# Residual, normalised and transposed rows and split latents moved by 64 bytes in on-chip memory, in a two-layer decoder trunk

## What is computed

```python
cond = jax.nn.silu(c)
for layer in range(DEPTH):
    mod = (cond @ ada_w[layer] + ada_b[layer])[:, None, :]
    sh_m, sc_m, g_m, sh_f, sc_f, g_f = jnp.split(mod, 6, axis=-1)
    h = _rmsnorm(x, gn[0]) * (1.0 + sc_m) + sh_m
    y = _stick_breaking(h, ...)      # layer 0;  _mla(h, ...) in layer 1
    x = x + g_m * _rmsnorm(y, gn[1])
    h = _rmsnorm(x, gn[2]) * (1.0 + sc_f) + sh_f
    y = _swiglu(h, ...)              # layer 0;  _moe(h, ...) in layer 1
    x = x + g_f * _rmsnorm(y, gn[3])
```

## Time and profile before

| | |
|---|---|
| runs | 819.71, 819.73, 819.80 us |
| profiled execution, span from first to last instruction | 818.9 us (its own time is not listed apart; the median of the runs is 819.73) |
| TensorE matmuls, busy | 796.3 us, 97% |
| weight loads / VectorE / ScalarE / GpSimd busy | 708.9 / 694.0 / 542.3 / 48.9 us |
| granted TensorE clock, mean | 0.994 of 2.4 GHz |
| DMA | 284.31 MB, mean 347 GB/s |

### The profile page before, as it was taken

One profiled execution on the slowest core, in us unless ns is written; L12 is line 12 of the kernel. 1 busy time (PEld: TensorE's weight loads), 2 busy tenths in 40 slices (PEclk: granted clock), 3 DMA queues, 4 the chain that ended last, 5 costly groups with the idle time before them and its releaser, 6 DMA issues.

```text
span 818.9 us, 12488 instructions
## 1 busy us (share of the span) xinstructions
PE 796.3 (97%) x4678; PEld 708.9 (87%) x4678; DVE 694.0 (85%) x587; ACT 542.3 (66%) x575; POOL 48.9 (6%) x54
## 2 busy tenths in 40 slices
PE   4999999999999999999999999999999999999995
PEld 4999788999999888999888888888888888888884
DVE  4998798789989886878479898988989898898998
ACT  5346846544343434767388797978788797878875
POOL 1000020011000300000012000000000000000120
PEclk9999999999999999999999999999999999999998
DMA  8999676499999997399929999999999999999992
GB/s 335 421 423 355 245 285 252 167 367 356 351 376 396 362 365 292 129 369 420 420 82 384 424 392 418 354 421 359 403 404 355 413 353 425 359 407 400 359 411 79
DMA packets 46793, 284.31 MB, mean 347 GB/s; under 512 B 6028, under 2 KB 6031, under 8 KB 21156
## 3 DMA queue, kind: packets, MB, share of 16 engines
q1 hardware_dynamic: 41002, 269.06, 84.1%
q0 software_dynamic: 3584, 12.60, 4.0%
q10 hardware_dynamic: 2170, 2.13, 0.8%
HBM read 258.09 MB, written 25.17 MB: 346 GB/s over the span
## 4 chain that ended last, share of the span: by engine, by line
PE 82%; DVE 5%; issue 4%; DMA 4%; ACT 3%; POOL 1%; SPq 0%; DVEq 0%; ACTq 0%; POOLq 0%
PE ps L2366 9%; PE ps L2362 8%; PE ps L2361 8%; PE ps L1854 7%; PE ps L1858 7%; PE ps L1862 7%; PE ps L2377 4%; PE ps L2378 4%; PE ps L2382 4%; PE ps L1790 3%; PE ps L1791 3%; PE ps L1792 3%; DMA ring<-in_ada_w 2%; PE ps L1809 1%; DVE w_lo L1118 1%
## 5 line engine op out<-in xcount | busy, mean ns | idle before, releaser
L1610 DVE TENSOR_TENSOR w_lo<-ring,w_hi 128x2048 fp32r<-128x2048 f32 (+1 forms) x96 | 210.0, 2200 | 29.7 <-ACT w_hi L953 29.4
L607 ACT ACTIVATE w_hi<-ring 128x2048 fp32r<-128x2048 f32 (+1 forms) x56 | 106.4, 1901 | 137.4 <-PE ps L1862 80.0
L953 ACT ACTIVATE w_hi<-ring 128x2048 fp32r<-128x2048 f32 (+1 forms) x96 | 174.9, 1840 | 8.9 <-PE ps L2366 8.9
L1118 DVE TENSOR_TENSOR w_lo<-ring,w_hi 128x2048 fp32r<-128x2048 f32 (+1 forms) x56 | 131.5, 2350 | 34.2 <-ACT w_hi L607 33.7
L1854 PE MATMUL ps<-hT_hi,w_hi 128*128 128x256 f32 x480 | 117.8, 282 | 0.0
L1858 PE MATMUL ps<-hT_lo,w_hi 128*128 128x256 f32 x480 | 117.1, 280 | 0.0
L1862 PE MATMUL ps<-hT_hi,w_lo 128*128 128x256 f32 x480 | 117.0, 280 | 0.0
L1610 DVE TENSOR_TENSOR m_lo<-ring,m_hi 128x1536 fp32r<-128x1536 f32 (+1 forms) x48 | 92.6, 1930 | 2.3 <-ACT m_hi L953 1.9
L2362 PE MATMUL ps<-w_hi,xe_lo 128*128 128x512 f32 (+1 forms) x256 | 92.3, 376 | 0.0
L2361 PE MATMUL ps<-w_hi,xe_hi 128*128 128x512 f32 (+1 forms) x224 | 85.2, 380 | 0.0
L1854 PEld LDWEIGHTS ps<-hT_hi,w_hi 128*128 128x128 f32 x480 | 83.5, 190 | 0.1
(11 more groups left out here) (407 smaller groups left out, 1466.9 us busy)
## 6 DMA issues: line engine op xcount, KB each, us to landing
ring<-in_moe_w_gu SPq DMA_DIRECT2D x64, 1024.0 KB, 6.9
ring<-in_ada_w SPq DMA_DIRECT2D x48, 1024.0 KB, 7.3
ring<-in_moe_w_down SPq DMA_DIRECT2D x32, 1024.0 KB, 7.2
ring<-in_moe_w_gu SPq DMA_DIRECT2D x32, 768.0 KB, 7.6
ring<-in_ffn_w_gu SPq DMA_DIRECT2D x22, 1024.0 KB, 6.2
ring<-in_sb_w_in SPq DMA_DIRECT2D x12, 1024.0 KB, 9.2
ring<-in_moe_w_down SPq DMA_DIRECT2D x16, 768.0 KB, 6.6
ring<-in_ffn_w_down SPq DMA_DIRECT2D x11, 1024.0 KB, 7.4
```

The lines of the kernel that those rows point to most:

```text
L607: act.activation(split_of(m)[0][:, 0:cols_n], ring[n % R][:, 0:cols_n], ACT.Copy).then_inc(hi_done, 1)
L953: act.activation(m_hi[k % NB][:, 0:n_c], ring[(N0 + k) % R][:, 0:n_c], ACT.Copy).then_inc(hi_done, 1)
L1118: dve.tensor_tensor(split_of(m)[1][:, 0:cols_n], ring[n % R][:, 0:cols_n], split_of(m)[0][:, 0:cols_n].bitcast(F32), ALU.subtract).then_in ...
L1610: dve.tensor_tensor(m_lo[k % NB][:, 0:n_c], ring[(N0 + k) % R][:, 0:n_c], m_hi[k % NB][:, 0:n_c].bitcast(F32), ALU.subtract).then_inc(free ...
```

## The change

Three pads and two offsets are changed. x, xhat, hT_hi and hT_lo, and what is laid on them (hid, qt, qnT, knT, y_of, gate_hi), lie 64 bytes lower; the third pad is 64 bytes longer, so gate, acc, base and the rest stay. cT_hi and cT_lo are moved 64 bytes lower within base. Modulo 512 these tensors stand at 448 in place of 0, which is 256 from w_hi and w_lo at 192. Nothing else is edited.

```diff
         cursor[0] += 192
         w_hi, w_lo = zip(*((sb(f"w_hi{b}", [P, PIECE], F32R), sb(f"w_lo{b}", [P, PIECE], F32R)) for b in range(2)))
         w_hi, w_lo = list(w_hi), list(w_lo)
-        cursor[0] += 320
+        cursor[0] += 256
         x = sb("x", [P, TC, D])
         xhat_at = cursor[0]
         xhat = sb("xhat", [P, TC, D])
         hT_at = cursor[0]
         hT_hi = sb("hT_hi", [P, DC, T], F32R)
         hT_lo = sb("hT_lo", [P, DC, T], F32R)
-        cursor[0] += 192
+        cursor[0] += 256
         gate = [sb(f"gate{w}", [P, D]) for w in range(2)]
...
-        cT_hi = sb("cT_hi", [P, 3, T], F32R, at=base + 9024)
-        cT_lo = sb("cT_lo", [P, 3, T], F32R, at=base + 12096)
+        cT_hi = sb("cT_hi", [P, 3, T], F32R, at=base + 8960)
+        cT_lo = sb("cT_lo", [P, 3, T], F32R, at=base + 12032)
```

## The result

After the change the kernel takes 822.91 us (median of six runs, 821.76 to 823.33) against 819.76 for the kernel before on the same chip (six runs, 819.50 to 821.05): ratio 1.003, 95% interval 1.002 to 1.0039. It is slower, by 0.3%. The profiled execution took 823.11 us.

What follows compares the result with a forecast made beforehand. TensorE, busy 97% of the span, was taken as the bound through its matmul start spacing. Terms +1.6 (slow narrow), +0.9 (fast narrow) and -0.3 us (wide) gave +2.2, so 821.9 us; own range 819.7 to 824.1, 8-in-10 range 811.0 to 824.5.

Steps and rivals of the forecast that it cites:

- the distance between starts: Back-to-back TensorE matmuls: time is their number times start spacing, changes reaching the end one for one; dense stage 118.8 ns.
- Distance, not place: Matmul operands: stationary minus moving address modulo 512 goes with the pace; 6.6 ns between distances 320 and 0.
- Nothing on VectorE and ScalarE: Instructions of these engines on the moved tensors cost nothing more; if wrong by 10 ns each, 1 us.
- The experts untouched: Expert stage: products with xe and eT stay at distance 0, so no change of pace.
- the extra at 256: Narrow and wide matmuls alike: 5.5 ns, middle of 4.4 and 6.6; terms +1.6, +0.9 and -0.3 us, sum +2.2.
- a circle of 512: Operand distances taken modulo 512, with 256 as far apart as possible, 64 bytes from neighbours 192 and 320.
- The gT row: Dense down projection, wide products with stationary gT: distance 0, settling at 226.7 ns against 233.3 at 320.
- Rival (a): Narrow and wide matmuls settle on the fast pace: 811.3 us, or 813.3 with narrow alone; chance 0.27.
- Rival (b): Only the wide matmuls gain, by 2.0 us: 817.7 us; chance 0.08.
- Rival (c): Addresses do nothing, the history of starts alone sets the matmul pace: 819.7 us; chance 0.08.
- Rival (d): Matmuls at 256 worse than both neighbours, 13.2 ns extra, 17 us more: 836.8 us; chance 0.05.

Runs made afterwards that it cites:

- abs256: Kernel before with w_hi, w_lo, gate, acc and base 64 bytes higher, rows and latents left in place (distance 256): 821.21 us, one run; before 820.49.
- dist0: Kernel before with pads and offsets putting rows and latents at the weights' 192 modulo 512 (distance 0): 821.96 us, one run; before 820.49.
- best320: dist320 again, the same program, timed in more rounds against the kernel before: median 815.15 us against 819.70, ratio 0.9952.
- dist128: Kernel before with pads and offsets putting rows and latents 128 bytes below the weights modulo 512: 820.61 us, one run; before 820.49.
- dist320: Kernel before with pads and offsets making weights minus rows and latents 320 modulo 512: 814.94 us, one run; before 819.72.

## Why the prediction came out right, and for what reasons it did not

The forecast was 821.9 us with 819.7 to 824.1 as its own range, and the time is 822.91 against 819.76: slower, by the distance between starts as named. That the size came out near the forecast is in part luck, as two of its terms were wrong in opposite directions.

- **That the distance between starts carries the time** held: dense stage +2.32 us, from 1056 intervals and nothing else. Only the sum treated all 1632 narrow intervals as lying on the path, and the 96 at 113.3 ns in the first two qkv pieces didn't, being ahead of the wait for VectorE's acc.
- **Distance, not place**: held (abs256). **Nothing on VectorE and ScalarE**: held, 693.2 against 694.0 us and 542.2 against 542.3. **The experts untouched**: held.
- **The term that failed is the extra at 256**, taken as 5.5 ns, the middle between neighbours on a circle of 512. There is no such circle. The period is 256, so that D = 256 equals 0. The narrow extra is 120.0 - 113.3 = 6.7 ns: +2.3 ns on the 1464 that had 117.7 in place of +1.1 (3.4 us in place of 1.6) and +6.7 on the other 168 (1.1 in place of 0.9). The wide extra is 0: -6.6 ns in place of -1.1 (-2.0 us in place of -0.3). That makes +2.5 against the +2.2 of the prediction. The two errors, +2.0 and -1.7, nearly cancelled. The sum was about right, but its terms weren't.
- **The gT row said so.** The prediction had distance 0 at the wide pace of 226.7 ns, and took it for the zero of all extras. For narrow products 0 is the dearest place (dist0, 120.0 ns). An extra read from one shape was carried over to another.
- **On the path** the stages give +2.32 (dense), +0.49 (qkv), +0.31 (MLA in), -0.65 (attention) and -0.41 (MLA attention), together +2.1 of the +2.4 in the span; the other 0.3 are nearly all in the start.
- **The other 0.8 us** between the medians aren't a matter of addresses as far as the runs show. The prediction took the 818.9 us of its profile for an execution of 819.73. But in every execution with both numbers on record the time is 1.7 to 1.8 us longer than the span, so that one took about 820.7 us (an estimate). In the 17 later runs of the kernel before (beside best320), nine with a mean granted clock of 0.996 to 0.998 take 819.27 to 819.70 us, and eight with 0.994 or 0.995 take 820.11 to 821.09. Of the six runs after, two with 0.996 and 0.997 take 821.76 and 822.06 us, and four with 0.995 take 822.71 to 823.33. At like clock the change costs some 2.3 us, an estimate over runs that may be of different chips. The rest of the 3.15 us goes with the clock: four of the six runs after had the lower one, and of the six before only one has such a time (821.05). Six runs can't tell whether the change has a part in that.
- **Rival (a)**, the steady fast pace, was wrong for this distance and right for another: 64 modulo 256. **Rival (b)**'s wide gain came (226.7 ns), but not alone. **Rival (c)**, that addresses do nothing, fell (the dense stage has 120.0 ns in dist0, 118.5 in dist128 and 113.3 in dist320). The Trainium skill ("TensorE: Matmul & The Clock Gate", step by step: what each phase is for) says that loading the next weights takes no read bandwidth from the running matmul. No run here measures read bandwidth, but the spacing doesn't follow from that sentence: moving the rows alone gives 113.3 ns (D = 64), 118.5 (128) or 120.0 (0) for the same matmuls. **Rival (d)**, an extra of 13.2 ns, appears nowhere.

**Open:** what decides between 113.3 and 117.8 ns at one address; why 64 and 192 differ; why 160 is as slow as 0 for narrow products; and whether hT in a copy of its own for each use (D = 64 for narrow products, 0 for wide ones) would give both gains, which wasn't tried. That the two read streams of TensorE meet in the memory is the explanation that fits; no run shows the conflict itself.

## What to carry to other kernels

Where TensorE runs back to back with a load for every matmul, take the pace from starts, and compare stationary and moving addresses modulo 256: here the narrow pace goes from 113.3 to 120.0 ns with nothing else changed. All of this was seen with operands of type float32r only. Try several distances for each shape, since the best for 512 columns (0) is, with 160, the worst for 256. Don't carry an extra from one shape to another, and don't read a period from two points.

## What was not expected of the hardware

- Two distances 256 apart give the same paces (0 and 256; 128 and 384) or the same pair of paces (64 and 320), and the sign matters: 121.13 us of dense stage at 64, 125.39 at 192.
- The order turns round with the width: at distance 0 the narrow pace is the slowest, with that at 160 (120.0 ns), and the wide one the fastest (226.7).
- At one address two paces, 113.3 and 117.8 ns, each hold for tens of microseconds, and in best320 the first passed into the second behind a wait of 0.3 us; in dist320, the same program, it did not.
- Behind the 16 one-column matmuls at 42 us (L1990, 1.92 us) the clock falls to 1.2 GHz in some executions (granted 0.76 before and 0.81 after, from 41 to 48 us) and not in others (1.00 in abs256), worth 1.1 us. In the kernel after it fell though TensorE didn't wait ahead of them.
